# A decoder block with 256 expert gathers on one core: slots two behind their dots, and the second tile's attention spread over more slots

## The reference

```python
mod = silu(c) @ w_ada + b_ada                  # six rows of 1024: sh1, sc1, g1, sh2, sc2, g2
h = x * (1 + sc1) + sh1
q, k, v = split(h @ w_in)                      # 16 heads of 64: 8 causal, 8 dilated windows
y = rms_norm(softmax(q k^T / 8 + bias) v) @ w_out
x = layer_norm(2**0.25 * x + (1 + g1) * y)
h2 = x * (1 + sc2) + sh2
for each token, for each of 8 heads:           # product keys: 128 x 128 = 16384 experts
    s1, s2 = halves of (h2 @ w_q) against two tables of 128 keys
    e, g = the 16 best sums s1[i] + s2[j] and their softmax
    f += sum over the 16: g * gelu(h2 . peer_u[e]) * peer_v[e]
x = layer_norm(2**0.25 * x + (1 + g2) * f)
```

## Time and profile before

| | us |
|---|---|
| median of 3 runs (lowest, highest) | 870.1 (868.52, 870.25) |
| profiled execution, its own time | 869.18 |
| its span | 867.3 |
| TensorE busy | 723.5 (83%) |
| VectorE busy | 566.1 (65%) |
| ScalarE busy | 343.5 (40%) |
| GpSimd busy | 277.2 (32%) |
| moved by the DMA engines | 327.95 MB, 268.45 of it by the 256 gathers |

### The profile page before, as it was taken

One profiled execution on the slowest core, in us unless ns is written; L12 is line 12 of the kernel. 1 busy time (PEld: TensorE's weight loads), 2 busy tenths in 40 slices (PEclk: granted clock), 3 DMA queues, 4 the chain that ended last, 5 costly groups with the idle time before them and its releaser, 6 DMA issues.

```text
span 867.3 us, 7303 instructions
## 1 busy us (share of the span) xinstructions
PE 723.5 (83%) x2042; PEld 341.5 (39%) x2042; DVE 566.1 (65%) x1289; ACT 343.5 (40%) x998; POOL 277.2 (32%) x260
## 2 busy tenths in 40 slices
PE   4999989877789899999997787878787777778874
PEld 2877844634344445444332232322222222223221
DVE  5674466777655867766675767876666667675554
ACT  0032031346552544353544535553434344443333
POOL 0000000123322364444434343445434434443430
PEclk9999989969989999999999999899999999999999
DMA  9999971599887999999999999999999999999992
GB/s 354 404 419 423 359 297 54 213 350 338 297 333 253 419 419 419 422 421 422 420 422 421 421 422 421 419 424 422 420 421 422 422 421 421 422 421 421 422 421 84
DMA packets 47895, 327.95 MB, mean 378 GB/s; under 512 B 5552, under 2 KB 7920, under 8 KB 8688
## 3 DMA queue, kind: packets, MB, share of 16 engines
q0 software_dynamic: 36864, 268.45, 75.6%
q1 hardware_dynamic: 8480, 56.70, 16.2%
q10 hardware_dynamic: 2512, 2.35, 0.8%
HBM read 326.40 MB, written 1.07 MB: 378 GB/s over the span
## 4 chain that ended last, share of the span: by engine, by line
DMA 47%; PE 28%; DVE 13%; ACT 7%; issue 3%; SPq 0%; DVEq 0%; POOL 0%; ACTq 0%
DMA ring<-in_experts,e_all 40%; PE bank L434 19%; DMA ring<-in_w 5%; PE bank L426 5%; DVE acc L846 5%; DVE ring L753 4%; ACT diag L605 2%; DMA skT<-in_skT 1%; ACT L597 1%; ACT weight L601 1%; ACT gel L597 1%; PE bank L477 1%; PE bank L512 1%; PE bank L531 1%; PE bank L568 1%
## 5 line engine op out<-in xcount | busy, mean ns | idle before, releaser
L434 PE MATMUL bank<-ring,diag 128*128 128x512 f32 x1024 | 511.8, 634 | 115.2 <-ACT diag L605 114.7
L963 POOL DMA_INDIRECT ring<-in_experts,e_all x256 | 277.0, 1082 | 562.7 <-PE bank L434 375.8
L434 PEld LDWEIGHTS bank<-ring,diag 128*128 128x128 f32 x1024 | 185.1, 196 | 416.7 <-ACT diag L605 252.3
L753 DVE CUSTOM_DVE_ANT_0 ring<-ring,T_h 128x1024 f32<-128x1024 f32 x128 | 156.7, 1225 | 113.3 <-DMA ring<-in_experts,e_all 113.3
L753 DVE CUSTOM_DVE_ANT_0 ring<-ring,h 128x1024 f32<-128x1024 f32 x128 | 156.2, 1222 | 73.9 <-DMA ring<-in_experts,e_all 73.8
L597 ACT ACTIVATE gel<-pre 128x1 f32<-128x1 f32 x256 | 51.6, 202 | 300.5 <-DVE pre L753 299.9
L605 ACT ACTIVATE diag<-consts,weight 128x128 f32<-128x128 f32 x256 | 102.8, 401 | 8.4
L601 ACT ACTIVATE weight<-gel,g_all 128x1 f32<-128x1 f32 x256 | 75.4, 295 | 9.6 <-ACT gel L597 0.4
L846 DVE SCALAR_TENSOR_TENSOR acc<-ring,cact,acc 128x512 f32<-128x512 f32 x84 | 63.2, 752 | 3.9 <-DMA ring<-in_w 0.2
L426 PE MATMUL bank<-ring,hT_yT 128*128 128x512 f32 x80 | 35.5, 594 | 0.0
L457 PE MATMUL bank<-hT_yT,lnw 128*128 128x256 f32 x128 | 31.0, 405 | 1.1 <-DVE hT_yT L830 1.1
(11 more groups left out here) (144 smaller groups left out, 550.9 us busy)
## 6 DMA issues: line engine op xcount, KB each, us to landing
ring<-in_w SPq DMA_DIRECT2D x34, 1024.0 KB, 11.7
lnw<-in_w SPq DMA_DIRECT2D x6, 1024.0 KB, 17.3
ring<-in_experts,e_all POOLq DMA_INDIRECT x256, 15.1
mod<-in_w SPq DMA_DIRECT2D x2, 1024.0 KB, 28.6
H_s<-scratch ACTq DMA_DIRECT2D x1, 2048.0 KB, 34.7
mod<-in_b_ada_r SPq DMA_DIRECT2D x1, 2048.0 KB, 25.2
lnw<-in_ln SPq DMA_DIRECT2D x1, 2048.0 KB, 10.7
xT_y<-in_xT SPq DMA_DIRECT2D x1, 1024.0 KB, 14.1
```

Source lines behind the costliest of these rows:

```text
L434: last = nc.tensor.matmul(tile_sum(t)[n], diag[:, i % DIAGS, :], ring[:, RING_AT[i], D + CH * n:D + CH * n + CH], start=(s == 0), stop=(s ...
L753: nc.vector.tensor_tensor_reduce(ring[:, r, 0:D], ring[:, r, 0:D], h2[i // SLOTS], 1.0, 0.0, ALU.mult, ALU.add, pre[:, i % PAIR:i % PAIR + ...
L963: nc.gpsimd.indirect_dma_start(ring[:, r, :], None, A["experts"], bass.IndirectOffsetOnAxis(ap=e_all[:, i:i + 1], axis=0)).then_inc(slot_i ...
```

## The change

- `LAG = 2`: `gather_steps(i)` ends with `slot` i - 2 in the place of `slot` i; the last two slots follow at the end.
- `BESIDE` is spread out: units 6 to 11 over slots 6 to 30 (before 1 to 19), units 4 and 5's later parts, which stood ahead of the first slot, at 0 to 2, `q`(0,2) at 34 (before 32), `wo` of tile 1 at 40 to 46 (before 22 to 28), its norm at 47 and 49 (before 29 and 31), `q`(0,3) at 55 (before 44), and the others of tile 1 later too.
- `S` 4 and 5 move behind the pieces of head 0.
- `wsum` 11, `modrow` 7 and `madd` 7 move from behind `v`(0,1) to far ahead: `wsum` 11 stands ahead of `wo`(0,0,1), `modrow` 7 behind `v`(1,1), `madd` 7 ahead of `q`(0,0). `wsum` 10 moves ahead of `S` 2 and 3, `madd` 2 ahead of `wsum` 8, `modrow` 6 ahead of `xa`. `ada` 11 is loaded behind `out` 0 and `x`, ahead of `q` 0, in `wring` 3 (before behind `v`(1,1), in `wring` 1); `q` 0 waits for `wsum` 11.
- The load of `x` moves behind `out` 0; the small loads `gn` and `skT` go from SP's queue to the start of ScalarE's.
- Three `qkz` move ahead of `wsum` 0 and `bias`.
- The ring begins with places 2, 3, 6, 7, 0, 1; a new `free` 0 behind `v`(1,1) gives places 2 and 3. Eight places are used from slot 54 on (before 36).

```diff
-          ("in", 3), ("in", 4), ("ada", 7), ("ada", 8), ("in", 5), ("ada", 9), ("ada", 10), ("out", 1), ("out", 0), ("q", 0),
-          ("ada", 11), ("q", 1)]
+          ("in", 3), ("in", 4), ("ada", 7), ("ada", 8), ("in", 5), ("ada", 9), ("ada", 10), ("out", 1), ("out", 0), ("ada", 11),
+          ("q", 0), ("q", 1)]
-W_PLACES = [0, 1, LN_PLACE, 2, 3, MOD_PLACE, 3, 1, 2, 0, 3, LN_PLACE, 1, 2, 1, 3, 2, LN_PLACE, 2, 3, 1]
+W_PLACES = [0, 1, LN_PLACE, 2, 3, MOD_PLACE, 3, 1, 2, 0, 3, LN_PLACE, 1, 2, 1, 3, 2, LN_PLACE, 2, 3, 3]
-NARROW = [6, 7, 0, 1, 2, 3]
+NARROW = [2, 3, 6, 7, 0, 1]
-WIDE_FROM = 36
+WIDE_FROM = 54
...
-    [("wsum", 0), ("bias",), ("modp", 0), ("qkz", 0, 0), ("qkz", 0, 1), ("qkz", 1, 0), ("qkz", 1, 1), ("wsum", 2), ("modc", 0), ("qkh", 0, 0), ("qkh", 0, 1), ("wsum", 1), ("modp", 1),
+    [("qkz", 0, 0), ("qkz", 0, 1), ("qkz", 1, 0), ("wsum", 0), ("bias",), ("qkz", 1, 1), ("modp", 0), ("wsum", 2), ("modc", 0), ("qkh", 0, 0), ("qkh", 0, 1), ("wsum", 1), ("modp", 1),
...
-       ("modrow", 0), ("madd", 0), ("modrow", 1), ("madd", 1), ("qk", 2, 1), ("yT", 0, 0), ("modrow", 2), ("wsum", 8), ("madd", 2),
-       ("qk", 3, 0), ("modrow", 3), ("madd", 3), ("qk", 3, 1), ("wsum", 9), ("S", 2), ("S", 3), ("modrow", 4), ("madd", 4),
-       ("v", 1, 0), ("wsum", 10), ("Tr", 2), ("Tr", 3), ("modrow", 5), ("wo", 0, 0, 1), ("madd", 5), ("PV", 2), ("PV", 3), ("ny", 0),
-       ("wo", 0, 0, 0), ("yT", 0, 1), ("xa", 0), ("modrow", 6), ("wo", 0, 1, 1), ("wo", 0, 1, 0), ("rows2",), ("madd", 6), ("ln1a", 0),
-       ("v", 1, 1), ("ln1b", 0), ("hT", 0, 0), ("hT", 0, 1), ("S", 4), ("S", 5), ("q", 0, 0), ("Tr", 4),
-       ("s", 0, 0, 0), ("s", 0, 0, 1), ("Tr", 5), ("q", 0, 1), ("s", 0, 1, 0), ("s", 0, 1, 1), ("PV", 4), ("PV", 5), ("v", 0, 1)]
+       ("modrow", 0), ("madd", 0), ("modrow", 1), ("madd", 1), ("qk", 2, 1), ("yT", 0, 0), ("modrow", 2), ("madd", 2), ("wsum", 8),
+       ("qk", 3, 0), ("modrow", 3), ("madd", 3), ("qk", 3, 1), ("wsum", 9), ("modrow", 4), ("madd", 4), ("wsum", 10), ("S", 2), ("S", 3),
+       ("v", 1, 0), ("modrow", 5), ("madd", 5), ("Tr", 2), ("Tr", 3), ("wsum", 11), ("wo", 0, 0, 1), ("PV", 2), ("PV", 3), ("ny", 0),
+       ("wo", 0, 0, 0), ("yT", 0, 1), ("modrow", 6), ("xa", 0), ("wo", 0, 1, 1), ("wo", 0, 1, 0), ("rows2",), ("madd", 6), ("ln1a", 0),
+       ("v", 1, 1), ("free", 0), ("modrow", 7), ("ln1b", 0), ("hT", 0, 0), ("hT", 0, 1), ("madd", 7), ("q", 0, 0),
+       ("s", 0, 0, 0), ("s", 0, 0, 1), ("q", 0, 1), ("s", 0, 1, 0), ("s", 0, 1, 1)]
+    + [("piece", 0, j) for j in range(PIECES)]
+    + [("free", 1), ("S", 4), ("S", 5), ("v", 0, 1), ("free", 2)]
-PLAN = PLAN[:-3] + [("piece", 0, j) for j in range(PIECES)] + [("free", 1)] + PLAN[-3:] + [("free", 2), ("wsum", 11), ("modrow", 7), ("madd", 7), ("free", 3)]
+LAG = 2
 BESIDE = {
-    1: [("S", 6), ("S", 7)], 3: [("Tr", 6), ("Tr", 7)], 5: [("PV", 6), ("PV", 7)], 7: [("yT", 1, 1)],
-    8: [("S", 8), ("S", 9)], 10: [("Tr", 8), ("Tr", 9)], 12: [("PV", 8), ("PV", 9)],
-    15: [("S", 10), ("S", 11)], 17: [("Tr", 10), ("Tr", 11)], 19: [("PV", 10), ("PV", 11)], 20: [("ny", 1)], 21: [("yT", 1, 0)],
-    22: [("wo", 1, 1, 1)], 24: [("wo", 1, 1, 0)], 25: [("xa", 1)], 26: [("wo", 1, 0, 1)], 28: [("wo", 1, 0, 0)], 29: [("free", 4), ("ln1a", 1)],
...
+    0: [("Tr", 4)], 1: [("Tr", 5)], 2: [("PV", 4), ("PV", 5)],
+    6: [("S", 6), ("S", 7)], 9: [("Tr", 6), ("Tr", 7)], 12: [("PV", 6), ("PV", 7)], 15: [("S", 8), ("S", 9), ("yT", 1, 1)],
+    18: [("Tr", 8), ("Tr", 9)], 21: [("PV", 8), ("PV", 9)], 24: [("S", 10), ("S", 11)], 27: [("Tr", 10), ("Tr", 11)],
+    30: [("PV", 10), ("PV", 11)], 31: [("ny", 1)], 32: [("yT", 1, 0)], 34: [("q", 0, 2)], 36: [("s", 0, 2, 0)], 37: [("s", 0, 2, 1)],
+    40: [("wo", 1, 1, 1)], 42: [("wo", 1, 1, 0)], 43: [("xa", 1)], 44: [("wo", 1, 0, 1)], 46: [("wo", 1, 0, 0)], 47: [("free", 4), ("ln1a", 1)],
+    49: [("ln1b", 1)], 51: [("hT", 1, 0)], 52: [("hT", 1, 1)],
...
-    return out + [("slot", i)]
+    return out + ([("slot", i - LAG)] if i >= LAG else [])
+PLAN += [("slot", NT * SLOTS - LAG + i) for i in range(LAG)]
...
-            sp.dma_start(x[:], A["x"].rearrange("(t p) c -> p t c", p=P)).then_inc(x_in, 16)
-            sp.dma_start(gn[:], A["gn"]).then_inc(gnsk_in, 16)
-            sp.dma_start(skT[:], A["skT"]).then_inc(gnsk_in, 16)
...
             load(("out", 0))
+            sp.dma_start(x[:], A["x"].rearrange("(t p) c -> p t c", p=P)).then_inc(x_in, 16)
+            summed(sp, 9)
+            load(("ada", 11))
+            summed(sp, 11)
             load(("q", 0))
-            filled(sp, ("v", 1, 1))
-            load(("ada", 11))
```

More of the change, by code:

```diff
@@ L90 @@
 PLAN = (
-    [("wsum", 0), ("bias",), ("modp", 0), ("qkz", 0, 0), ("qkz", 0, 1), ("qkz", 1, 0), ("qkz", 1, 1), ("wsum", 2), ("modc", 0), ("qkh", 0, 0), ("qkh", 0, 1), ("wsum", 1), ("modp", 1),
-     ("qkh", 1, 0), ("wsum", 3), ("modc", 1), ("qkh", 1, 1), ("qk", 0, 0), ("qk", 0, 1), ("qk", 1, 0), ("qk", 1, 1), ("wsum", 4)]
+    [("qkz", 0, 0), ("qkz", 0, 1), ("qkz", 1, 0), ("wsum", 0), ("bias",), ("qkz", 1, 1), ("modp", 0), ("wsum", 2), ("modc", 0), ("qkh", 0, 0), ("qkh", 0, 1), ("wsum", 1), ("modp", 1),
+       ("qkh", 1, 0), ("wsum", 3), ("modc", 1), ("qkh", 1, 1), ("qk", 0, 0), ("qk", 0, 1), ("qk", 1, 0), ("qk", 1, 1), ("wsum", 4)]
     + [("tflip", j) for j in range(8)]
     + [("wsum", 5), ("wsum", 6), ("S", 0), ("S", 1), ("v", 0, 0), ("Tr", 0), ("Tr", 1), ("wsum", 7), ("qk", 2, 0), ("PV", 0), ("PV", 1),
-       ("modrow", 0), ("madd", 0), ("modrow", 1), ("madd", 1), ("qk", 2, 1), ("yT", 0, 0), ("modrow", 2), ("wsum", 8), ("madd", 2),
-       ("qk", 3, 0), ("modrow", 3), ("madd", 3), ("qk", 3, 1), ("wsum", 9), ("S", 2), ("S", 3), ("modrow", 4), ("madd", 4),
[4 rows of a table removed]
+       ("modrow", 0), ("madd", 0), ("modrow", 1), ("madd", 1), ("qk", 2, 1), ("yT", 0, 0), ("modrow", 2), ("madd", 2), ("wsum", 8),
+       ("qk", 3, 0), ("modrow", 3), ("madd", 3), ("qk", 3, 1), ("wsum", 9), ("modrow", 4), ("madd", 4), ("wsum", 10), ("S", 2), ("S", 3),
[4 rows of a table added]
+    + [("piece", 0, j) for j in range(PIECES)]
+    + [("free", 1), ("S", 4), ("S", 5), ("v", 0, 1), ("free", 2)]
 )
-PLAN = PLAN[:-3] + [("piece", 0, j) for j in range(PIECES)] + [("free", 1)] + PLAN[-3:] + [("free", 2), ("wsum", 11), ("modrow", 7), ("madd", 7), ("free", 3)]
 HEAD1 = [(0,), (1, 2), (3,), (4, 5), (6,), (7,), (8,), (9, 10), (11,)]
+LAG = 2
 BESIDE = {
[7 rows of a table removed]
-} | {84 + 2 * i + z: [("s", 1, i, z)] for i in range(4) for z in range(2)}
[8 rows of a table added]
+} | {88 + 2 * i + z: [("s", 1, i, z)] for i in range(4) for z in range(2)}
 def gather_steps(i):
@@ L578, in _ @@
             nc.scalar.dma_start(consts[:], A["consts"]).then_inc(consts_in, 16)
+            nc.scalar.dma_start(gn[:], A["gn"]).then_inc(gnsk_in, 16)
+            nc.scalar.dma_start(skT[:], A["skT"]).then_inc(gnsk_in, 16)
             act.wait_ge(set_ready, 1)
@@ L677, in _ @@
                 elif kind == "free":
-                    if step[1] == 1:
+                    if step[1] == 0:
+                        filled(act, ("v", 1, 1))
+                        act.sem_inc(ring_free, 2)
+                    elif step[1] == 1:
                         filled(act, ("q", 0, 1))
@@ L683, in _ @@
                         filled(act, ("v", 0, 1))
-                        act.sem_inc(ring_free, 2)
-                    elif step[1] == 3:
-                        summed(act, 11)
                         act.sem_inc(ring_free, 2)
```

## The result

| | before | changed |
|---|---|---|
| median us (lowest, highest), 4 runs each | 869.42 (868.52, 870.25) | 861.94 (861.0, 862.67) |
| profiled execution, its span | 869.18, 867.3 | 862.67, 860.9 |
| first gather issued, us | 166.65 | 180.35 |
| from there to the end of the span, us | 700.65 | 680.55 |

The ratio is 0.9914 (95% interval 0.9896 to 0.9931): faster by 7.5 us, where 17 were forecast. The last two lines of the table split the error. From the first gather on the changed kernel is 20.1 us faster (forecast 19.9). But the first gather comes 13.7 us later (forecast 2.7). The whole miss lies ahead of the gathers.

A forecast was written before the change was run, and what follows sets the result against it. DMA transfers bound it: bytes plus holes, from waiting for the first gather and from the ring. Span 867.3 + 2.7 - 19.9 = 850.1, plus 2.8 gives 852.9, so 853 us; range 846 to 864.

The forecast's parts named there:

- Edits ahead of 102 us: Before 102 us: early `qkz`, small loads on ScalarE's queue and `madd` 2 ahead of `wsum` 8 are worth nothing by themselves.
- sign of being wrong: Forecast is wrong if the first gather is beyond 173 or share from there to slot 54 is under 0.9.
- Term A: Way to the first gather: it starts 2.7 us later, at 169.3 instead of 166.65; bounds +0.3 and +6.
- the cost of the clock: Behind TensorE's idle time before `yT`(0,1): the lowered clock costs 2.3 us, now on `wo`(0,1,1).
- the wait eats what is gained: Before `yT`(0,1): `wsum` 11's wait for `ada` 11 delays `PV` 2 and 3, eating all 6.4 us gained.
- Term B: After the first gather: 28.9 us of transfer holes shrink to 9, so -19.9 us; what stays is 4 to 22.
- The argument from load: First 36 slots: 99 us of TensorE against 99.6 of transfers leave no room; spread over 54 slots, 134 against 144.5.
- R1: Slots after unit pairs: ScalarE's chain is too long, holes return at pairs and `wo`; 859 to 866 us; 20%.
- R2: Gather ring: the lag holds places two slots longer, six act as four; 870 us; 5%.
- R3: Gather ring: six places starve to slot 54, making the kernel slower, 887 us; 7%.
- R4: Before the first gather: a longer `ada` 11 wait eats the ring's gain, first gather near 186, nothing changes; 4%.
- The start of the slots: First slots: slot 0 done at 185 to 186.5, gathers in flight last to 186.1; 2 us hole.

The follow-up runs named there:

- `qkz` back: The changed kernel with the three early `qkz` put back behind `modp` 0: 851.09 us, ratio 0.9789, first gather at 168.46.
- dense: Changed kernel, three `qkz` put back, lag 2, units 6 to 11 and following work at the before kernel's slots, eight places from slot 36: 850.07 us, ratio 0.9801.
- LAG 0: The changed kernel with the three `qkz` put back and LAG = 0, slot i again directly behind dot i: 863.45 us, ratio 0.9944.
- LAG 1: The changed kernel with the three `qkz` put back and LAG = 1: 855.07 us, ratio 0.9838.

## Why the prediction was wrong

- **The failed step: "Edits ahead of 102 us ... Worth nothing by themselves."** It argued that where the transfers are full an earlier TensorE is worth nothing, and took full transfers for fixed landings. They were full in both kernels while the table was under way, but shared otherwise: what SP's queue gained by coming 2.2 us earlier the table on the other queue lost. This step is the whole miss: without the early `qkz` the kernel takes 851.09 us, where 853 was forecast. The step cost 11.9 us of first gather (180.35 against 168.46) and 10.8 us of time (861.94 against 851.09). No rival named it. The profile of the kernel before had the warning: the table took 34.7 us for 2 MB, where 421 GB/s would take 5.0, and landed only 4.3 us before TensorE came for it. The forecast's own sign of being wrong, a first gather beyond 173, came true.
- **Term A** otherwise: +2.7 forecast, +1.8 measured with the `qkz` back. With the `qkz` back the landing of `ada` 11 (126.66, forecast 126.5), TensorE's stand (6.03, forecast 5.8) and the cost of the clock (0.5 on `yT`, 0.9 on `modrow` 6 and 0.9 on `wo`(0,1,1), forecast 2.3 in all) were right to a few tenths. That the wait eats what is gained was right, and moving the load gave the 7.6 us.
- **Term B**: -19.9 forecast, -20.1 measured in the changed kernel. The size was right and half of its argument wrong. The lag took away stands and clock dips, as said. The argument from load (99 us of TensorE against 99.6 of transfers, so "no room") did not hold: dense work with the lag is as fast, and in the kernel before with LAG = 2 TensorE is busy 105.7 of 116 us with 36 slots and the same work beside them, and the transfers still run at a share of 0.98. (The sum of 99 us was also set beside the wrong stretch: the earlier trace rows's third held 28 slots, not 36.) Without the lag the rest is 693.5 with all else changed, against 700.65 before; that may be the spreading or the ring's new order, which no run parts. With the lag the spreading gives nothing that the runs show (679.6 against 677.6 dense).
- **Rivals**: R1 (ScalarE's chain too long), R2 (places held longer) and R3 (six places starve) would show in the rest of the span, and it is where it was forecast. R4 was the right kind, a first gather near 186 that eats the gain, for the wrong reason and at 4%.
- **The start of the slots**: forecast was slot 0 done 15.7 to 17.2 us after the first gather's issue and a hole of 2 us. In the changed kernel the seventh gather, which waits for slot 0, is issued at 197.89, 17.5 us after the first, and the transfers run at 385 GB/s over the first 40 us: (1 - 385/421) x 40 = 3.4 us, the largest hole left.
- **The range** of 846 to 864 held the time, on its slow side, by a mechanism that it did not contain: that was luck.

## What to carry to other kernels

A transfer in small packets on a second queue gets its turn by packets, so its landing depends on when the other queue runs dry; before making the big queue busier, look who shares the engines with it. In an in-order plan, put the consumer one or two steps behind its producer before spreading work out: the lag alone gave all that the spreading was meant for. And a full resource is no proof that an edit ahead of it is free.

## What the hardware showed that I had not expected

- Two queues at work shared the DMA engines by packets, 194 to 194 in 4 us, and so 1.44 MB to 0.20 MB. The same 2048 KB took 26.5, 34.7 or 47.1 us, as the other queue stood empty near 40 us for about three us, about two, or not at all.
- A stand of TensorE of 3.3 to 3.6 us is followed by a pair of slots of 5.40 us instead of 3.6. Three of them are 3 x (3.5 + 1.8) = 15.9 us of TensorE, beside the 12.4 us of time that LAG 0 costs; how much of the 12.4 each stand costs, the runs do not part. Not every stand does it: with LAG 1 one of 3.68 us was followed by a slot at full clock (1.98 us).
